# Chunk stage of an RWKV-7 mixer: another order in the fill and the first step, and the scaling of keys ahead of the second mask half

## The reference, cut to what matters

```python
def step(S, inp):
    r_t, w_t, k_t, v_t, a_t, b_t = inp
    sa = jnp.einsum('bhij,bhj->bhi', S, a_t)
    S = (S * w_t[:, :, None, :] + sa[..., None] * b_t[:, :, None, :]
         + v_t[..., None] * k_t[:, :, None, :])
    return S, jnp.einsum('bhij,bhj->bhi', S, r_t)
...
_, y = lax.scan(step, S0, seq_in)
```

## Time and profile before

| | |
|---|---|
| Time, median of 3 runs | 1500.68 us (1496.58 to 1503.44) |
| The profiled execution's own time | 1501.69 us |
| Its span in the trace | 1500.0 us |
| Busy: PE, DVE, ACT, POOL | 1429.8, 1029.7, 740.7, 95.2 us |
| Mean granted TensorE clock | 0.985 |
| Fill of the chunk stage, first PE row | 877.18 us |
| First row of step 1 on PE | 936.94 us |
| Last steps end, about | 1056 us |

### The profile page before, as it was taken

The page is one execution under the profiler, slowest core; times in us unless marked ns, Lnnn a source line. Parts: engine busy times, 40 slices in busy tenths (PEclk is TensorE's granted clock), DMA queues, the critical chain, the costliest instruction groups (busy, mean ns, idle before and its releaser), DMA issues.

```text
span 1500.0 us, 30264 instructions
## 1 busy us (share of the span) xinstructions
PE 1429.8 (95%) x12891; PEld 1315.4 (88%) x12891; DVE 1029.7 (69%) x1463; ACT 740.7 (49%) x1071; POOL 95.2 (6%) x122
## 2 busy tenths in 40 slices
PE   6999999999999999998999986999799999999997
PEld 5998898999999999998999775888367998899986
DVE  5666567588843787577968775786678883488732
ACT  4555465454532455458578542443455552255422
POOL 3010011000030000000000141110000000000010
PEclk9999999999999999999999997999999999999998
DMA  4212221423433333555322233332332343333331
GB/s 131 64 58 64 65 64 57 113 85 99 123 88 88 92 104 96 141 156 195 89 61 78 85 75 57 57 62 44 111 99 85 104 119 106 95 87 111 87 97 56
DMA packets 283990, 136.78 MB, mean 91 GB/s; under 512 B 65449, under 2 KB 278593, under 8 KB 283601
## 3 DMA queue, kind: packets, MB, share of 16 engines
q1 hardware_dynamic: 283552, 134.77, 32.6%
q10 hardware_dynamic: 304, 0.08, 0.0%
HBM read 124.33 MB, written 10.49 MB: 90 GB/s over the span
## 4 chain that ended last, share of the span: by engine, by line
PE 78%; DVE 11%; ACT 6%; DMA 3%; issue 2%; SPq 0%; DVEq 0%; ACTq 0%
PE psg L1883 26%; PE psx L1724 13%; PE psg L1724 11%; PE psg L2689 9%; PE psg L591 2%; DVE w_lo L137 2%; PE psx L591 2%; PE psg L619 2%; PE psg L675 1%; ACT rest_hi L331 1%; DVE rest_lo L430 1%; DVE sum_lo L447 1%; PE psx L3398 1%; ACT rest L317 1%; ACT rest L323 1%
## 5 line engine op out<-in xcount | busy, mean ns | idle before, releaser
L133 ACT ACTIVATE w_hi<-w_raw 128x1024 fp32r<-128x1024 f32 (+1 forms) x122 | 142.0, 1165 | 209.6 <-PE psg L1883 147.9
L1883 PE MATMUL psg<-mid_hi_l,w_hi 128*128 128x264 f32 (+1 forms) x720 | 232.8, 323 | 2.9 <-DVE w_lo L137 2.0
L1883 PE MATMUL psg<-mid_lo_l,w_hi 128*128 128x264 f32 (+1 forms) x720 | 231.6, 322 | 0.0
L1883 PE MATMUL psg<-mid_hi_l,w_lo 128*128 128x264 f32 (+1 forms) x720 | 231.0, 321 | 0.0
L137 DVE TENSOR_TENSOR w_lo<-w_raw,w_hi 128x1024 fp32r<-128x1024 f32 (+1 forms) x121 | 165.0, 1364 | 77.7 <-ACT w_hi L133 77.1
L1883 PEld LDWEIGHTS psg<-mid_hi_l,w_hi 128*128 128x128 f32 x720 | 135.3, 188 | 14.7 <-DVE w_lo L137 2.6
L1883 PEld LDWEIGHTS psg<-mid_lo_l,w_hi 128*128 128x128 f32 x720 | 135.3, 188 | 10.5 <-issue 0.2
L1883 PEld LDWEIGHTS psg<-mid_hi_l,w_lo 128*128 128x128 f32 x720 | 135.4, 188 | 10.3
L2689 PE MATMUL psg<-x_hi,w_hi 128*128 128x264 f32 (+1 forms) x320 | 99.8, 312 | 7.9 <-DVE w_lo L137 7.9
L2689 PE MATMUL psg<-x_lo,w_hi 128*128 128x264 f32 (+1 forms) x320 | 98.8, 309 | 0.0
L2689 PE MATMUL psg<-x_hi,w_lo 128*128 128x264 f32 (+1 forms) x320 | 98.6, 308 | 0.0
(11 more groups left out here) (518 smaller groups left out, 4324.2 us busy)
## 6 DMA issues: line engine op xcount, KB each, us to landing
w_raw<-in_w_ffn_out_dram SPq DMA_DIRECT2D x40, 704.0 KB, 4.7
w_raw<-in_w_qkv_dram SPq DMA_DIRECT2D x24, 512.0 KB, 3.7
w_raw<-in_w_rkv_dram SPq DMA_DIRECT2D x24, 512.0 KB, 3.9
x_raw_l<-in_w_ffn_in_dram SPq DMA_DIRECT2D x18, 512.0 KB, 4.1
x_raw_l<-in_w_ffn_in_dram SPq DMA_DIRECT2D x36, 256.0 KB, 4.7
w_raw<-in_w_ffn_in_dram SPq DMA_DIRECT2D x16, 512.0 KB, 3.9
y_raw_l<-in_w_ffn_in_dram SPq DMA_DIRECT2D x16, 512.0 KB, 4.0
y_raw_l<-in_w_ffn_in_dram SPq DMA_DIRECT2D x32, 256.0 KB, 4.6
```

Source lines behind the costliest of these rows:

```text
L133: k.nc.scalar.activation(k.w_hi[j][:, 0:kt, :], k.raw[j][:, 0:kt, :], ACT.Copy).then_inc(k.hi_ready[j].h, 1)
L1883: done = k.nc.tensor.matmul(self.bank(i, c), w[:, t, :], x, start=t == 0 and n == 0, stop=t == count - 1 and n == 2)
```

## The change

It moves calls inside `chunk_stage`; no operation is added or taken out. The one difference in size is that the `keep` matmuls of fill and step 0 go from 96 to 76.

- DVE: `products(2)` and `keys(0, 0)` go ahead of the lane operations of chunk 0. Step 0 becomes `first_step`, which begins with the lane operations of chunk 2. In steps 1 to 4 `products(c + 4)` goes ahead of the masks of the second half.
- PE: `quads(0, 1)` and `l_products(2)` go ahead of the 44 `keep` matmuls; 36 others are gone. In step 0 both halves of `quads(1, ...)` stand around `chain_u`, ahead of `chain_s`; 16 `keep` matmuls are added there.
- ACT: `values_turned(0, 0)` ahead of `decays(2)`; `lower(2)`, `decays(3)` and the gate split ahead of `av_out(0, 0)`.
- SP: `keep_low(2)` ahead of `keep_inverse(0)`, `fetch_lanes(2)` right behind it. `keep_low(n)` waits for one lane fetch more than before.

```diff
@@ sync(sp)
             def keep_low(n):
                 sp.wait_ge(low_r.h, n + 1)
                 if n >= 2:
-                    sp.wait_ge(lane_in.h, 16 * (n - 1))
+                    sp.wait_ge(lane_in.h, 16 * n)
...
+            keep_low(2)
             sp.wait_ge(inv_in.h, 64)
             for n in range(CHUNKS):
                 if 1 < n < CHUNKS - 1:
                     keep_low(n + 1)
                     fetch_lanes(n + 1)
                 keep_inverse(n)
+                if n == 0:
+                    fetch_lanes(2)
                 fetch_inverse(n)
-                if n == 1:
-                    keep_low(2)
-                    fetch_lanes(2)
@@ scalar(act)
+                if n == 3:
+                    act.wait_ge(low_out.h, 32)
...
             keys_turned(0, 0)
+            values_turned(0, 0)
             decays(2)
             lower(1)
-            values_turned(0, 0)
+            lower(2)
+            decays(3)
             end_decay(0, 0)
-            av_out(0, 0)
             act.wait_ge(g_in.h, (1 + P // G_REST) * 16)
             nc.scalar.activation(r.g_hi[:], r.g_raw[:], ACT.Copy).then_inc(g_split.h, 1)
-            lower(2)
-            decays(3)
+            av_out(0, 0)
@@ vector(dve)
+            def first_step(n, p, q):
+                small_blocks(2)
+                last_blocks(2)
+                keys(n, 0)
+                reads(n, p, 0)
+                products(3)
+                keys(n, 1)
+                reads(n, p, 1)
+                grow(q, 0)
+                next_t(n)
+                dve.wait_ge(g_split.h, 1)
+                nc.vector.tensor_tensor(r.g_lo[:], r.g_raw[:, 0], r.g_hi[:, 0].bitcast(F32), ALU.subtract)
+                next_xt(n, p, 0)
+                next_xs(n, p)
+                next_xt(n, p, 1)
+                nc.vector.tensor_tensor(r.g_hi[C:P, 1], r.g_raw[C:P, 1], r.g_hi[C:P, 1].bitcast(F32),
+                                        ALU.subtract).then_inc(g_split.h, 1)
+                products(4)
+                small_blocks(3)
...
                     keys(n, 0)
                     reads(n, p, 0)
+                if c + 4 < CHUNKS:
+                    products(c + 4)
+                if prep:
                     keys(n, 1)
                     reads(n, p, 1)
                     next_xt(n, p, 1)
-                if c + 4 < CHUNKS:
-                    products(c + 4)
                 if c + 3 < CHUNKS:
                     small_blocks(c + 3)

             products(1)
+            products(2)
+            keys(0, 0)
             small_blocks(0)
             last_blocks(0)
-            keys(0, 0)
             keys(0, 1)
             small_blocks(1)
             last_blocks(1)
-            products(2)
@@ tensor(pe)
                 if c == 0:
                     turn_bk(n)
+                    keep(8)
                     turn_v(n)
+                    keep(8)
+                    quads(n, 0)
                     chain_u(c, q)
+                    quads(n, 1)
                     chain_s(c, q)
-                    quads(n, 0)
...
-                    quads(n, 1)
+                    if c:
+                        quads(n, 1)
...
             keep(8)
+            turn_v(0)
             l_products(1)
-            turn_v(0)
             quads(0, 0)
+            quads(0, 1)
+            l_products(2)
             keep(44)
-            quads(0, 1)
             a_v(0, 0)
-            keep(36)
-            l_products(2)
```

More of the change, by code:

```diff
@@ L3295, in step @@
                     nc.vector.tensor_scalar(wt[:], av[q][:], -1.0, None, ALU.mult).then_inc(wt_r.h, 1)
[L3296 to L3301, removed]
+                    first_step(n, p, q)
+                    return
                 if not prep:
@@ L3306, in step @@
                     next_t(n)
-                if c == 0:
+                if c + 2 < CHUNKS:
+                    last_blocks(c + 2)
+                if prep:
                     next_xt(n, p, 0)
                     next_xs(n, p)
[L3310 to L3316, removed]
                     grow(q, c)
-                if prep:
                     keys(n, 0)
                     reads(n, p, 0)
+                if c + 4 < CHUNKS:
+                    products(c + 4)
+                if prep:
                     keys(n, 1)
```

## The result

The changed kernel takes 1490.58 us (median of 9 runs, 1488.93 to 1496.20), the kernel before 1503.18 us in the same comparison (9 runs). The ratio is 0.9926, 95% interval 0.9911 to 0.9940: 11 us less (9 to 13 by the interval; the two medians lie 12.6 apart). The forecast was 12.0 us less, 1488.7 us. Disturbed runs are left out of every ratio in this document.

The account below looks back on a forecast made before the run. Fill and step 0 were bound by DVE idling, then making PE wait; steps 1 to 4 by PE, but for 1.15 us waits. 9.3 + 2.7 = 12.0 off 1501.7 gave 1489.7, less 1.0 for the median 1488.7 us; range 1483 to 1497.

Parts of the forecast that it names:

- The fill and the masks: Fill and start of step 0: DVE's masks of chunk 1 end at 910.4, against 930.16 before.
- the 0.7 us allowed: Fill: extra time in all for DVE's lane operations of chunks 0 and 1 running beside GpSimd's products(3).
- Masks to step 1: Step 0 from the masks' end at 910.4 to step 1 at 928.5, which then begins 8.4 us earlier than before.
- the gate split: End of step 0: gate newly waits for the split behind next_xt on DVE, 2.3 us, from 923.9 to 926.2.
- the clock: Step 0: PE at half clock behind the masks, full clock back at 919.7, ahead of gate, 9.3 us behind R.
- R: The time when DVE's masks of chunk 1 are ready in step 0: forecast 910.4, against 930.16 before.
- the 1.1 us that I counted as saved: First two groups of step 1 at full clock: 0.8 and 0.3 us saved.
- Steps 1 to 4: The wait of l_products for DVE goes: two steps save 1.15 us, two about 0.2, together 2.7.
- the counterweight: Steps 1 to 4: xs transfers through memory, slack 0.2 and at most 0.6 us, limit two steps' saving to about 0.2.
- slower: Rival, chance 0.04: chunk 2's lanes land late behind keep_low(2) and DVE waits in step 0; slower from a landing at 922.
- no gain: Rival, chance 0.06: another path, such as fetch_inverse(1), sets step 0's end; 1496 to 1499 us.
- The low-clock rival: Rival, chance 0.17: clock low through step 0 and transfers take the steps' gain; 6.3 us saved, 1494.4.

Follow-up runs that it names:

- e9_no_keep_in_fill: The changed kernel without the 44 keep matmuls between l_products(2) and a_v(0, 0) in the fill; ratio 0.9934 to the kernel before.
- e3_fill_only: The fill of the changed kernel, with step 0 and the later steps as in the kernel before; ratio 0.9988 to the kernel before.
- e8_clock_kept: The kernel of e7_all_three plus 22 keep matmuls in four PE rests behind the masks of step 0; median 1484.51 us, ratio 0.9890.
- e1_scaling_only: The kernel before, with only DVE's products(c + 4) moved ahead of the second mask half in steps 1 to 4; ratio 0.9969.
- e7_all_three: The changed kernel with early gate split, 44 keep matmuls in step 0's PE hole, and xs on its own semaphore; median 1487.53 us, ratio 0.9890.

## Why the prediction came out as it did

**The fill and the masks: right, by small errors that cancel.** Masks 33.2 us into the stage were forecast, 33.4 measured. The lanes beside GpSimd cost more than the 0.7 us allowed: chunk 0's took 885.47 to 893.29 = 7.8, chunk 1's 7.1, against 6.64 each, so 1.7 in all. (The lanes of chunk 0 in the kernel before, 885.36 to 892.88, already took 7.5; the 6.64 is that of chunk 1.) In return the lanes of chunk 0 began 0.4 us earlier in the stage than forecast, and the masks between them, `wt` and the lanes of chunk 2 each took 0.1 or 0.2 less. That these came to 0.8 is luck. `av_out` ended at 897.14, 3.7 us ahead of `wt`, so the forecast that it just meets DVE had it too close, at no cost. `e9_no_keep_in_fill` shows that the 44 `keep` matmuls that are left in the fill neither cost nor give; that the 36 that went cost nothing is not shown. `e3_fill_only` shows that the fill alone is worth 3.2 us of the 7.4 up to step 1. The rest comes with the order of step 0, on DVE and PE together; no run parts these two.

**Masks to step 1: 18.1 forecast, 18.8 measured.** The waits came as foreseen, 2.07 for the 2.3 of the gate split; the 0.14 us that I allowed twice for a semaphore stand in no row, and the rows show 0.04 (922.08 to 922.12) and 0.06 (924.09 to 924.15). The mistaken step is the clock. I had it back 9.3 us behind R and then up through `gate`, `a_v` and step 1. It was back after 5.4 us and lost again at 921.2. The 9.3 was read at one place and taken as fixed; in the same trace PE resumed at 908.29, behind a rest of 2.23 us, and the clock was at 1.00 again from 912.2 on, 3.9 us later. So the rows right behind R cost less than forecast (6.9 us up to `times_x` for 7.6), those from `gate` on more (3.6 for 2.3), and the 1.1 us that I counted as saved in the first two groups of step 1 were not: 1.96 as before, and 1.91 for 1.39. This is the term that was sized wrongly, 9.3 forecast for this part against 7.4 measured. `e8_clock_kept` prices what the second fall costs, 2.1 to 2.5 us, on top of the other three edits and by one profile.

**Steps 1 to 4: 2.7 forecast, 3.2 and 4.3 measured** in the two profiles, 3.5 in `e1_scaling_only`. The forecast also held the `times_x` of chunk 6, which stands behind the four steps; with what lies there, 2.7 and 4.0 were measured. The mechanism holds: the wait of 1.15 us is gone, and the counterweight is there, with 0.54 us of waiting for `xs` in the four steps of one profile and 0.20 and 0.38 behind them. But I took the two slow trips of the kernel before for a property of chunks 4 and 6. They move from profile to profile; steps 2 to 4 together lost 1.1 us in one profile of the change and nothing in the other. The three rows name `xs`, the last issue, as what they waited for; `e7_all_three` and `e8_clock_kept`, with `xs` apart, waited for `xt` (0.90, and 0.28 and 0.47 us), so the last issue is not the only late one.

**The sum.** 9.3 + 2.7 = 12.0 forecast; 7.4 + 3.2 - 0.4 = 10.1 in the stage of the first profile, 11.5 in the second, about 11 by the timing. The 12.0 lies inside the 9 to 13 of the timing, which can't tell it from 10.1. The rivals: "slower" by a late lane fetch didn't come (`lane_low` for chunk 2 was issued at 895.16, some 6 us ahead of its first use); "no gain" by another path neither. The low-clock rival was half right: the clock was low from 921.2 on, but not throughout, and the transfers took about 1 us in one profile and nothing in the other.

## What to carry to other kernels

Look for an engine that idles first and is then waited for: the idle time is where its late work belongs, and moving work there pays, if its data arrive through an earlier queue entry. It does not pay by the length of the hole: here DVE's 10.49 us of idle time went, the masks came 19.6 us earlier, and step 1 began 7.4 us earlier, because the state sums and `l_products(3)` now stand behind the masks. Then follow what the newly exposed stretch does to the engine behind. In short rests of PE the array fell to half clock; 22 idle matmuls in just these rests gave 2 us back by the profile, while 44 in the fill gave nothing. Measure a stage from its own first instruction: here its start moved by 7 us between profiles of code that is the same up to there.

## What the runs showed of the hardware

- A fall to 1.2 GHz follows not only one long rest. In the changed kernel it came at 921.2, behind rests of 0.62, 1.17 and 0.56 us and before the rest of 2.07 at `gate`; in `e8_clock_kept`, with these rests filled, the granted clock stayed 1.00.
- DVE and GpSimd wait for each other, one whole instruction at a time. GpSimd's two products of chunk 2 in the changed kernel, and the two of step 0 beside `g_lo` (917.31 to 919.35):

```profile
882.63 1.76 POOL L3149 TENSOR_TENSOR bk_late<-rows,w_inv 128x512 f32<-128x512 f32 x1 [0.81 <-ACT w_inv L3059]
884.36 1.71 POOL L3150 TENSOR_TENSOR rows<-rows,w_inv 128x512 f32<-128x512 f32 x1
...
917.00 1.27 POOL L3149 TENSOR_TENSOR bk_late<-rows,w_inv 128x512 f32<-128x512 f32 x1 [22.55 <-ACT w_inv L3059]
918.23 2.25 POOL L3150 TENSOR_TENSOR rows<-rows,w_inv 128x512 f32<-128x512 f32 x1
```

  Alone they take 1.26, DVE's product 0.68 and `g_lo` 1.22. DVE's second product (883.19, 1.75 us) ended 0.55 us behind GpSimd's first; `g_lo` (2.04 us) ended 1.08 behind the row that began at 917.00; GpSimd's last row, of 2.25 us, ended 1.13 behind `g_lo`. Each ends about its own length alone behind the other's end.
- The stores of the inverted blocks (L3010, 64 KB each) landed 2.5 to 4.5 us after their issue in the kernel before and 2.5 to 4.3 in the changed one; the `xs` fetches of the changed kernel took 3.0 to 4.5.
